# The first modulation's scale half loaded ahead of its shift half, and the first three tiles computed from the scaled raw input

## The reference

```python
mod = silu(c) @ w + b                      # w: 1024 x 3072
shift, scale, gate = split(mod, 3)
h = rms_norm(x) * (1 + scale) + shift
x = x + gate * f(h)
```

## Time and profile before

| | |
|---|---|
| median of 3 runs | 1299.44 us (1298.76 to 1301.04) |
| the profiled execution's own time | 1300.4 us |
| its span in the profile | 1298.2 us |
| TensorE busy | 1259.0 us (97%) |
| VectorE busy | 847.2 us (65%) |
| ScalarE busy | 540.2 us (42%) |
| GpSimd busy | 30.8 us (2%) |
| mean DMA traffic | 119 GB/s, 154.42 MB |

### The profile page before, as it was taken

The page is one execution under the profiler, slowest core; times in us unless marked ns, Lnnn a source line. Parts: engine busy times, 40 slices in busy tenths (PEclk is TensorE's granted clock), DMA queues, the critical chain, the costliest instruction groups (busy, mean ns, idle before and its releaser), DMA issues.

```text
span 1298.2 us, 17924 instructions
## 1 busy us (share of the span) xinstructions
PE 1259.0 (97%) x6179; PEld 984.7 (76%) x6179; DVE 847.2 (65%) x1284; ACT 540.2 (42%) x983; POOL 30.8 (2%) x39
## 2 busy tenths in 40 slices
PE   5999999999999999999999999999999999999997
PEld 3677777676888878888888666667788888888886
DVE  3656756766888888855547767765776666664332
ACT  5544444534333333332235566664543333332222
POOL 2000000000000000000020000000300000000000
PEclk8999999999999999999999999999999999999998
DMA  9623433342566656556532111123233333333332
GB/s 308 192 66 97 139 101 107 111 146 49 195 195 195 195 188 194 168 165 209 164 98 60 38 34 36 34 59 93 70 102 95 97 96 96 97 93 105 90 90 93
DMA packets 241012, 154.42 MB, mean 119 GB/s; under 512 B 38153, under 2 KB 232174, under 8 KB 237882
## 3 DMA queue, kind: packets, MB, share of 16 engines
q1 hardware_dynamic: 240954, 153.63, 39.6%
HBM read 151.47 MB, written 2.14 MB: 118 GB/s over the span
## 4 chain that ended last, share of the span: by engine, by line
PE 87%; DVE 6%; ACT 2%; SPq 2%; issue 1%; DMA 1%; POOL 0%; DVEq 0%; ACTq 0%; POOLq 0%
PE pj L1679 74%; PE ov L1962 3%; PE sc L1906 3%; PE tr L1934 3%; PE sc L1918 1%; DVE wl L1134 1%; SPq L530 1%; DVE tmp L1228 1%; ACT wh L711 1%; DMA first_ada<-in_ada_w_dram 1%; DVE nmax L1297 1%; PE ov L1847 1%; DVE hl L1209 0%; PE sc L1924 0%; ACT tmp L861 0%
## 5 line engine op out<-in xcount | busy, mean ns | idle before, releaser
L1134 DVE TENSOR_TENSOR wl<-raw,wh 128x1024 fp32r<-128x1024 f32 (+2 forms) x214 | 236.1, 1103 | 264.2 <-ACT wh L711 261.0
L711 ACT ACTIVATE wh<-raw 128x1024 fp32r<-128x1024 f32 (+2 forms) x214 | 204.4, 955 | 456.8 <-PE pj L1679 456.8
L1679 PE MATMUL pj<-hh,wh 128*128 128x512 f32 x944 | 377.0, 399 | 6.4 <-issue 3.1
L1679 PE MATMUL pj<-hh,wl 128*128 128x512 f32 x944 | 368.2, 390 | 0.0
L1679 PE MATMUL pj<-hl,wh 128*128 128x512 f32 x944 | 367.8, 390 | 0.0
L1679 PE MATMUL pj<-gh,wh 128*128 128x512 f32 x560 | 223.0, 398 | 1.1 <-DVE rope_sb L1597 0.5
L1679 PE MATMUL pj<-gh,wl 128*128 128x512 f32 x560 | 219.3, 392 | 0.0
L1679 PE MATMUL pj<-gl,wh 128*128 128x512 f32 x560 | 218.7, 391 | 0.0
L1679 PEld LDWEIGHTS pj<-hh,wh 128*128 128x128 f32 x944 | 177.4, 188 | 48.7 <-issue 10.2
L1679 PEld LDWEIGHTS pj<-hh,wl 128*128 128x128 f32 x944 | 177.3, 188 | 37.8
L1679 PEld LDWEIGHTS pj<-hl,wh 128*128 128x128 f32 x944 | 177.6, 188 | 33.6 <-DVE hl L1209 0.2
(11 more groups left out here) (216 smaller groups left out, 1048.2 us busy)
## 6 DMA issues: line engine op xcount, KB each, us to landing
raw<-in_ffn_w_in_dram SPq DMA_DIRECT2D x88, 512.0 KB, 3.8
ada_w_sb<-in_ada_w_dram SPq DMA_DIRECT2D x40, 1024.0 KB, 5.2
raw<-in_ffn_w_out_dram SPq DMA_DIRECT2D x32, 448.0 KB, 3.4
raw<-in_fox_w_in_dram SPq DMA_DIRECT2D x24, 512.0 KB, 3.8
first_ada<-in_ada_w_dram SPq DMA_DIRECT2D x16, 512.0 KB, 8.9
raw<-in_ffn_w_out_dram SPq DMA_DIRECT2D x16, 512.0 KB, 3.6
raw<-in_fox_w_o_dram SPq DMA_DIRECT2D x8, 512.0 KB, 3.7
raw<-in_mla_w_o_dram SPq DMA_DIRECT2D x8, 512.0 KB, 3.7
```

What stands on the lines that cost most here:

```text
L711: act.activation(wh[:, n0 % 2, 0:kt, :], raw[:, n0 % 2, 0:kt, :], ACT.Copy).then_inc(w_hi, 1)
L1134: dve.tensor_tensor(wl[:, n0 % 2, 0:kt, :], raw[:, n0 % 2, 0:kt, :], f32(wh[:, n0 % 2, 0:kt, :]), ALU.subtract).then_inc(w_lo, 1)
L1679: ins = pe.matmul(bank_[:, :], (wl if term == 2 else wh)[:, s, kt, :], (rl if term == 1 else rh)(kt), start=start and j == 0, stop=stop an ...
```

## The change

- The four blocks are now 512 columns of one half each: blocks 0 and 1 are the scale, blocks 2 and 3 the shift, in two transfers of 1 MB with runs of 2 KB. q's chunk and the gate's weights are loaded behind block 0, k's chunk behind block 1, v's and the second pair's q behind block 3. q and k have room of their own for their raw weights. Transfers for the taps wait until block 3 has been multiplied, the next modulation part for the gate's shift product.
- The squares are made half on ScalarE (tiles 0 to 3) and half on VectorE (4 to 7), and TensorE sums them over features directly: for each tile four products with one moving column, 32 in all. The sum on VectorE is gone, and ScalarE loads its square root table ahead of x.
- As soon as the scale of a tile is there, ScalarE and VectorE make the high and low part of x * (1 + scale), without root and shift, and TensorE multiplies them by q's, the gate's and k's weights.
- The root is multiplied on later: on the gate's logits by VectorE, on q and k by GpSimd. The shift comes as `shift @ w`: 8 fp32 products for the gate and 16 for q and k, with the weights loaded and one moving column.
- v's tile still takes the full h. For it x * (1 + scale) * root is made by VectorE for tiles 0 to 3 and by GpSimd, in two operations each, for tiles 4 to 7.
- A block has four columns of tiles to turn in place of two times two, by four products with one moving column.
- The cumulated sum takes one scan where it took a subtraction and a scan, and one copy where it took two.

The core of the diff, TensorE's and GpSimd's lists first:

```diff
             def block_rows(b):
...
-                pe.wait_ge(ada0_in[b], 16 * 4)
-                for kt in range(0, DT, 2):
-                    for side in range(2):
-                        for odd in range(2):
-                            at = 32 * (2 * side + odd)
-                            ins = pe.matmul(block_psum(b)[at:at + 1, :], csil[:, kt + odd:kt + odd + 1],
-                                            first_w[:, b, kt + odd, side, :], start=kt == 0, stop=kt == DT - 2)
+                pe.wait_ge(ada0_in[b], 16 * 2)
+                for k0 in range(0, DT, 4):
+                    for q in range(4):
+                        ins = pe.matmul(block_psum(b)[32 * q:32 * q + 1, :], csil[:, k0 + q:k0 + q + 1],
+                                        first_w(b)[:, k0 + q, :], start=k0 == 0, stop=k0 == DT - 4)
...
                 for j in range(BT):
-                    ins = pe.matmul(block_turned(b)[:, j:j + BT + 1:BT], block_row_sb(b)[:, j * P:(j + 1) * P], pick[:, :],
+                    ins = pe.matmul(block_turned(b)[:, j:j + 1], row_w[:, j * P:(j + 1) * P], pick_all[:, :],
                                     start=True, stop=True)
...
+            def first_square(at):
+
+                kt = FIRST_SQ[at]
+                if kt < 4:
+                    pe.wait_ge(sq, kt + 1)
+                else:
+                    pe.wait_ge(sq_v, kt - 3)
+                for b in range(QB):
+                    ins = pe.matmul(OV[0][:, b:b + 1], first_sq[kt][:, b * P:(b + 1) * P], inv_n[:, 0:1],
+                                    start=at == 0 and b == 0, stop=at == DT - 1 and b == QB - 1)
+                ins.then_inc(mean if at == DT - 1 else sq_used, 1)
+
+            def first_shift(to, weight, kt):
+
+                ins = pe.matmul(to, weight, mod[:, 0, kt:kt + 1], start=kt == 0, stop=kt == DT - 1)
+                return ins
...
+            for at in range(4):
+                first_square(at)
             block_rows(0)
-            norm(0, 0)
+            for at in range(4, DT):
+                first_square(at)
+            pe.wait_ge(pick_ok, 2)
+            turn_block(0)
+            spread(0)
+            for kt in range(4):
+                first_product(0, kt)
+                f_product(kt)
             block_rows(1)
-            spread(0)
...
+            turn_block(1)
+            first_product(0, 4)
+            f_product(4)
+            first_product(0, 5)
+            f_product(5)
             block_rows(2)
+            first_product(0, 6)
+            f_product(6)
+            first_product(0, 7)
+            turn_block(2)
+            f_product(7)
+            for kt in range(5):
+                first_product(1, kt)
+            block_rows(3)
+            for kt in range(5, DT):
+                first_product(1, kt)
+            turn_block(3)
+            pe.wait_ge(block_ok, BLOCKS)
+            pe.wait_ge(block_sb, BLOCKS)
+            for kt in range(DT):
+                ins = first_shift(SC[1][0:HEADS, 0:1], f_raw[:, kt, :], kt)
+            ins.then_inc(f_shift, 1)
+            for j in range(2):
+                for kt in range(DT):
+                    ins = first_shift(SC[0][:, j:j + 1], raw_tile(j)[:, kt, :], kt)
+            ins.then_inc(qk_shift, 1)
+            pe.wait_ge(z_t, 1)
+            for kt in range(DT):
                 pe.wait_ge(h_lo, kt + 1)
...
+                product(C_FOX + 2, 0, 0, 3 * kt, 3 * kt + 3, h_h, h_l, PJ[(T_FOX + 2) % 2])
             taps()
-            pe.wait_ge(cum_ok, 2)
+            pe.wait_ge(cum_ok, 1)
...
+            pool.wait_ge(rb_copy, 1)
+            for kt in range(4, DT - 1):
+                first_rooted(kt)
+            pool.wait_ge(block_ok, 2)
+            pool.wait_ge(pre, 4)
+            for kt in range(4, DT - 1):
+                first_scaled(kt)
+            pool.wait_ge(f_mm, 1)
+            first_rooted(DT - 1)
+            first_scaled(DT - 1)
+            z_scaled(0)
+            z_scaled(1)
...
+            act.activation(rb_sb, OV[1][:, :], ACT.Copy).then_inc(rb_copy, 1)
+            first_high(2)
+            first_high(3)
+            act.activation(early[:, 7:8], eps[:, 0:1], ACT.Exp)
+            split(C_FOX + 1)
+            block_take(1)
             act.wait_ge(block_ok, 2)
...
+            block_mod(0)
+            norm(0)
+            split(C_FOX)
+            dve.wait_ge(block_ok, 1)
+            first_lows((0,))
             dve.wait_ge(f_hi, 1)
             dve.tensor_tensor(f_wl[:, :, :], f_raw[:, :, :], f32(f_wh[:, :, :]), ALU.subtract).then_inc(f_lo, 1)
-            split(C_FOX)
-            modulated(0, 0)
...
+            first_lows((1, 2, 3))
+            dve.wait_ge(rb, 1)
+            for kt in range(4):
+                dve.scalar_tensor_tensor(out=first_pre(kt), in0=xT[:, kt, :], scalar=mod[:, 0, DT + kt:DT + kt + 1],
+                                         in1=OV[1][:, :], op0=ALU.mult, op1=ALU.mult).then_inc(pre, 1)
             split(C_FOX + 1)
+            block_mod(1)
+            dve.wait_ge(block_ok, 2)
+            first_lows(range(4, DT))
```

More of the change, by code:

```diff
@@ L73 @@
 N_CKV, N_CQ, N_FINAL = 3, 4, 6
-SSQ_TILES = (DT, DT - 1, DT - 1, KVRT, QRT, DT - 1, DT - 1)
-SSQ_END = [sum(t + 1 for t in SSQ_TILES[:n + 1]) for n in range(len(SSQ_TILES))]
+SSQ_TILES = (0, DT - 1, DT - 1, KVRT, QRT, DT - 1, DT - 1)
+SSQ_END = [sum(t + 1 for t in SSQ_TILES[1:n + 1]) for n in range(len(SSQ_TILES))]
 AW = 2 * D
@@ L135, in slot_count @@
 def slot_count(n):
-    return 16 * sum(slot_loads(c) for c in range(n % 2, n + 1, 2))
+    return 16 * sum(slot_loads(c) for c in range(n % 2 + 2, n + 1, 2))
 def build(nc, x, c, ada_w, ada_b, fox_w_in, fox_b_f, fox_w_o, mla_w_a, mla_g_q, mla_g_kv,
@@ L216, in u_tile, with first_u, first_pre, raw_tile @@
             return tile(gh if high else gl, m + DT)
+        def first_u(kt, high):
+            return tile(gh if high else gl, kt)
+        def first_pre(kt):
+            return (mid if kt < 4 else soft)[:, (8 + kt % 4) * S:(9 + kt % 4) * S]
+        def raw_tile(n):
+            if isinstance(n, int) and n < 2:
+                return (mid, soft)[n][:, 12 * S:14 * S].rearrange("p (t q) -> p t q", q=P)
+            return raw[:, n % 2, :, :]
         def h_tile(k, kt, high):
@@ L294, in build @@
         vT = tmp[:, 2, :]
-        fga = [tmp[0:HEADS, i, :] for i in range(6)]
+        fga = [tmp[0:HEADS, i, :] for i in (0, 1, 2, 3, 2)]
         F_PSUM = OV[0]
@@ L328, in build @@
         raw_in = [sem(f"raw_in{i}") for i in range(2)]
+        first_in = [sem(f"first_in{i}") for i in range(2)]
         w_hi = sem("w_hi")
@@ L1230, in modulated @@
                                              op0=ALU.mult, op1=ALU.mult).then_inc(pre, 1)
-                    if kt and (k or kt not in (4, 6)):
+                    if kt:
                         low(kt - 1)
@@ L1248, in _ @@
+            dve.wait_ge(x_e, 2 * QB)
+            for kt in range(4, DT):
+                first_square(kt)
             dve.wait_ge(consts, 6)
             dve.tensor_tensor(pick[:, :], ident[:, 0:P:HD], ident[:, HD // 2:P:HD], ALU.add).then_inc(pick_ok, 1)
-            block_shift_scale(0)
+            dve.wait_ge(pick_ok, 1)
+            dve.tensor_tensor(pick_all[:, :], pick[:, 0:1], pick[:, 1:2], ALU.add).then_inc(pick_ok, 1)
+            block_mod(0)
+            norm(0)
+            split(C_FOX)
```

296 lines of the change are left out of this document (167 added, 129 removed).

## The result

The changed kernel takes 1314.95 us (1313.73 to 1319.1), where the kernel before took 1300.22 in the same comparison: a ratio of 1.0124, 95% interval 1.0107 to 1.0141. It is slower by about 15 us. That was forecast as to its sign (+7.1), and the range ended 3 us short of it. The profiled execution took 1313.74 us with a span of 1311.9, 13.7 more than before.

A forecast was written before the change was run, and what follows sets the result against it. Transfers bound the kernel up to 35.67 us, then TensorE's own work. Products starting at 26.6 plus 39.75 us put the scores at 66.3 (+4.85); two clock falls add 2.25: +7.1, 1306.5 us, range 1298.8 to 1312.0.

The forecast's parts named there:

- Three blocks of sums and three turns: TensorE work behind the first q product: blocks 1 to 3 at 1.84 us each, 5.5; turns at 0.9 each, 2.7.
- signs named for being wrong: Mean before 21 us, shift products under 3 us, TensorE waiting for block 1, 2 or 3, or a difference arising behind 70.
- the term for the clock: Falls to half clock around block 0's turn and spread, and around block 1's turn; 2.25 us more with both.
- the 96 products: Products between the first q product and the scores, same as before: 0.227 us each, 21.8 us.
- the 16-column passes: In the later shift, 8 products with 16 loaded columns: 16 passes at 0.08 us, 1.3 us.
- the waits: TensorE waits around block 1's turn (0.85 and 2.45 us) and before the shift products (0.5), together 3.8 us.
- the cumulated sum: Before the scores, the gate's cumulated sum ends later than TensorE, behind ScalarE's other work: 0.7 us.
- single-column products don't count as work for the clock: Rival, 0.13: half clock from about 17 to 34 us; scores at 73.7, +12.3, 1311.7 us.
- Around 304 us they do no harm: Evidence cited against the rival that single-column products don't count as work: such products near 304 us.
- nearest of the four: Cases: forecast 0.45 (+7.1); no clock fall 0.22 (+4.85); single-column products not counted as work 0.13 (+12.3); not slower 0.20 (-0.5).
- The fourth rival: Not slower, 0.20: one-moving-column products at half price in mean, turns and shift; scores at 60.8 to 61.1, -0.5 us.
- the lower end of the range: 1298.8 us for the whole run, taken down to the not-slower case, whose time was put at 1298.9.

The follow-up runs named there:

- combo1: The changed kernel with the mean by VectorE's sum, block 1 ahead of tile 2, and the shift sums with the weights moving; 1305.6 us, ratio 1.005.
- early1: The changed kernel with block 1's sums behind the second tile's products and its turn behind the third's, engine orders matched; 1311.71 us.
- b_narrow: The kernel before with 48 unused fp32 products of 128 loaded columns and one moving, between v's chunk and the taps; 1320.04 us, ratio 1.0158.
- b_wide: The kernel before with 48 unused fp32r products of 128 loaded and 512 moving columns between v's chunk and the taps; 1310.33 us, ratio 1.0081.
- shift_one: The changed kernel with only one of eight feature tiles in the shift products, 3 products in place of 24; 1314.72 us, ratio 1.0118.
- shift_rows: The changed kernel with the shift column loaded and the weights moving, then a copy by ScalarE and three turning products; 1315.68 us, ratio 1.0129.
- sq_wide: The changed kernel with seven tiles' squares as fp32 products of 512 moving columns, result unused; 1315.81 us, ratio 1.0128.
- shift_fill: The changed kernel with 18 wide products, result unused, put among the 24 shift products; 1323.73 us, ratio 1.0194.

## Why the prediction was wrong in size

**Right.** Transfers are off the path, and TensorE's work in a row bounds the entry. Three blocks of sums and three turns lie behind the start (1.87 + 1.83 + 1.83 and 1.07 + 0.79 + 0.80 us, against 5.5 and 2.7). A wait stands behind block 1's turn, and a stretch at half clock behind it. GpSimd's work reaches nobody. What comes behind 77 us is moved by a constant, but for the 1.9 us told above. None of the signs named for being wrong came; it was the places, the lengths and the number of the clock's falls that missed.

**The step that failed** is the term for the clock. "In the new order two places are thin", 2.25 us in all. Four stretches came, 27.2 us long, two of them in work without a gap, and every price of the sum that stands in one was taken at full clock. Piece by piece, measured less full-clock price:

- mean and block 0: squares 5.55 - 3.6 = 1.95, block 3.24 - 1.84 = 1.4, squares 4.16 - 3.6 = 0.56, turn 1.72 - 0.9 = 0.8, spread 2.08 - 1.0 = 1.1. Together 5.8.
- the 96 products: 6.37 + 4.58 + 2.27 + 4.14 + 2.27 + 8.22 = 27.85 on the chain, against 21.8: 6.05. Some 0.4 of it is there at full clock too (2.27 for nine), which leaves 5.65; 2.8 of that is v's chunk alone.
- the shift: 6.40, of which 0.55 are the 16-column passes, against 0.55 + 3.6: 2.25.

The sum is 13.7 us, and half of the 27.2 us at half clock is 13.6. I had 2.25. The difference, 11.4, is larger than the miss (13.7 against 7.1 in the span), because other terms were too high: 1.15 between turn and first product, where VectorE's split and low part lay under the slow spread; 1.0 in the waits; 0.7 for the cumulated sum; 0.75 for the 16-column passes; and the 1.9 behind the scores, 5.5 in all. Against them stand 0.3 for the later start of the squares and the 0.4 of the products: 11.4 - 5.5 + 0.7 = 6.6. At full clock throughout, TensorE's own work would put the scores near 77.1 - 13.7 = 63.4, only 1.9 later than before. That is an estimate, and ScalarE's chain would stop it: it ended 11.2 us behind block 3's addition (62.1 to 73.3), which by the same sums would fall to 53.5, so the scores could not come ahead of some 64 to 65. combo1, at full clock from 28 us on, had them at 65.53.

**How it was reasoned.** The mechanism that the runs bear out was on the list, as the rival that "single-column products don't count as work for the clock", at 0.13 and with +12.3. The evidence against it was misread. "Around 304 us they do no harm" was two groups of eight passes between wide products, which says nothing of 32, and in the same trace the clock fell at 307.1, behind them and a wait of 0.71 us (columns as in the earlier trace rows):

```profile
307.50:310.70 3.20, 3.20 (x11) 2.40 (x10) 2.05 (x3) 1.33 (x2) 0.00 (x0) 0.53 0.54 161
```

The changed kernel has the same passes there and no fall, so that place speaks neither for nor against. The fall at 23.81 in the earlier trace rows came behind the mean's eight passes and a wait of 1.16 us, so it could not tell the two causes apart, yet it was given to the waits. That rival had the clock return once the q products ran and never fall again. It did fall again, in the shift, and took 5 us there. Its 1311.7 us was the nearest of the four, still 3.2 us short: none of the four had the clock fall in the shift.

**The fourth rival** (half the price in a row) is out: 32 passes take 3.9 us where the clock was full for most of them (early1), 0.12 each. Its own sum does not come out either: it names savings of 3.6, 1.35 and 2.4 us, which from 66.3 lead to 59.0 (59.5 if block 0 is there only at 16.5) and not to 60.8 or 61.1. So the lower end of the range, which was taken from it, was not what its terms give (-2.4 us, 1297.0).

**The 16-column passes** took 0.55 us for 16 (the timeline above), 0.035 each. I had put 1.3 in all. The Trainium skill (TensorE: Matmul & The Clock Gate, LDWEIGHTS) has the loading time go with the loaded columns. By that rule alone 16 passes would cost an eighth of 0.112 each, 0.22 in all (an estimate), and not the 0.4 of the prediction. The trace has a third of 0.112 for an eighth of the columns: it agrees in the direction, and its 0.55 lies above both.

**How far the runs bear this out.** That a long row of narrow passes brings the fall with no wait near is shown by b_narrow beside b_wide. That the stretch in the shift and v's chunk goes with them is shown by shift_one and shift_rows. For the mean it is shown in part: sq_wide has the clock back at 18.25 and none of the half clock from there to the first products, but in both kernels the clock fell first soon behind a wait of 1.4 to 1.5 us. In early1, with the same front, it fell only at 18.0 and again at 25.0, with TensorE at work in the squares and block 0 from 14.82 on. The fall at 43.5 goes with a wait (early1). What stays open is whether one moving column or the load in front of each is what counts, and what makes a given fall come when it does: the same 32 passes took from 3.9 to 6.9 us in five kernels whose front is the same. Whether 512 moving columns of squares against one loaded column, which would give the mean as a row, keep the clock up was not tried.

## What to carry to other kernels

Count a matmul by what it does to the clock as well as by its time. Here the clock fell in long rows of products with 128 loaded columns and one moving, with TensorE busy throughout, and the wide products behind them paid too: 48 cost 20 us where their own time is 10.8. Before such work is moved onto the path, swap its sides so that the many columns move (the shift went from 6.40 to 1.15 us, with a copy and three small turns to add), or leave it to an engine that is waiting anyway. And when a wait is taken away, follow the next chain to its end before counting the gain: both runs with a shorter shift gained nothing: TensorE then waited 3.4 and 4.1 us for ScalarE's chain, and the clock fell behind that wait.

## What the runs showed that was not expected

- Wide products between narrow ones did not lift the clock: 13.5 us at half with TensorE busy throughout, two wide products (1.06 us) behind every eight passes (1.50 us), and 17.25 us at half in shift_fill.
- The clock also fell where no narrow pass stood near: in the kernel before at 866.9 us, behind 863.45 to 866.85 with TensorE busy for 1.61 of 3.40 us and no single wait over 1.55.
- A plain fp32 product of 512 columns with 128 loaded takes 0.89 us, 0.446 a pass, while four with one loaded column, on four column groups, take 0.97 together.
- GpSimd's multiply of 512 columns by one value per partition takes 1.9 us, longer than its product of two tiles. Three of each, in its timeline:

```profile
32.31 4.70 POOL L715 TENSOR_TENSOR soft<-xT,diag 128x512 f32<-128x512 f32 x3 [23.48 <-ACT diag L874]
41.86 5.73 POOL L720 TENSOR_SCALAR soft<-soft,mod 128x512 f32<-128x512 f32 x3 [4.85 <-DVE mod L1284]
```

- Beside the first of them VectorE's low parts took twice as long, beside the second they did not (VectorE's timeline, two and four of them):

```profile
32.87 2.98 DVE L1334 SCALAR_TENSOR_TENSOR gl<-xT,mod,gh 128x512 fp32r<-128x512 f32 x2 [0.77 <-ACT gh L842]
...
42.62 3.09 DVE L1334 SCALAR_TENSOR_TENSOR gl<-xT,mod,gh 128x512 fp32r<-128x512 f32 x4 [0.86 <-ACT gh L842]
```
